# GpSimd subtracts the low half of a gate unit in four operations of two k tiles instead of one over eight

## What is computed

```python
proj = h @ w_in                                   # 1024 x 4772
c_q, c_kv, k_r, fq, fk, fv, f_logit, u, gate_logits = jnp.split(proj, split_points, axis=-1)
o_mla = causal_block_attention(q_mla, k_mla, v_mla)
o_fox = causal_block_attention(q_fox, k_fox, v_fox, cum_log_f)
o_s5 = s5_branch(u, ...)
branches = jnp.stack([o_mla, o_fox, o_s5], axis=2)
gates = jax.nn.sigmoid(gate_logits.reshape(bsz, seq, N_BRANCHES, D_MODEL))
projected = jnp.einsum('bsnw,nwd->bsnd', branches, w_branch)
merged = jnp.einsum('bsnd,bsnd->bsd', gates, projected)
return merged @ w_out
```

## Time and profile before

| | us |
|---|---|
| median of 3 runs (1450.96 to 1451.15) | 1451.15 |
| the profiled execution | 1450.45 |
| its span | 1448.4 |
| TensorE busy | 1429.4 (99%) |
| VectorE busy | 984.3 (68%) |
| ScalarE busy | 664.5 (46%) |
| GpSimd busy | 158.1 (11%), of it line 739: 60.0 |

### The profile page before, as it was taken

The page is one execution under the profiler, slowest core; times in us unless marked ns, Lnnn a source line. Parts: engine busy times, 40 slices in busy tenths (PEclk is TensorE's granted clock), DMA queues, the critical chain, the costliest instruction groups (busy, mean ns, idle before and its releaser), DMA issues.

```text
span 1448.4 us, 19055 instructions
## 1 busy us (share of the span) xinstructions
PE 1429.4 (99%) x7078; PEld 1202.5 (83%) x7078; DVE 984.3 (68%) x1432; ACT 664.5 (46%) x1076; POOL 158.1 (11%) x163
## 2 busy tenths in 40 slices
PE   9999999999999999999999999999999999999998
PEld 7999988888788888888888888888888888888887
DVE  6213556646866557839827688877778886678886
ACT  6231455646445542136512455555555555544332
POOL 1000610112361112103100000000000000000000
PEclk9999999999999999999999999999999999999999
DMA  7102021150121133337561222222222222890222
GB/s 267 64 0 102 19 74 44 52 164 24 46 60 52 37 88 95 82 134 249 185 222 54 88 73 88 87 88 82 71 82 88 88 88 89 318 387 35 95 74 80
DMA packets 130438, 148.94 MB, mean 103 GB/s; under 512 B 11370, under 2 KB 95261, under 8 KB 130077
## 3 DMA queue, kind: packets, MB, share of 16 engines
q1 hardware_dynamic: 130160, 147.68, 30.8%
q10 hardware_dynamic: 189, 0.08, 0.0%
HBM read 110.83 MB, written 36.31 MB: 102 GB/s over the span
## 4 chain that ended last, share of the span: by engine, by line
PE 90%; DVE 5%; ACT 2%; DMA 1%; issue 1%; POOL 1%; SPq 1%; ACTq 0%; DVEq 0%
PE ps L2215 29%; PE ps L693 14%; PE ps L2522 5%; PE ps L2524 5%; PE ps L2523 5%; PE ps L2613 4%; PE ps L374 3%; PE ps L375 3%; PE ps L376 3%; PE ps L882 2%; PE ps L3093 2%; PE ps L3094 2%; PE ps L3095 2%; PE ps L1524 2%; PE ps L861 2%
## 5 line engine op out<-in xcount | busy, mean ns | idle before, releaser
L2215 PE MATMUL ps<-split_arena 128*128 128x512 f32 x1320 | 306.8, 390 | 0.0
L693 PE MATMUL ps<-split_arena 128*128 128x512 f32 x1152 | 290.3, 399 | 2.2 <-ACT plain_arena L728 2.2
L2215 PEld LDWEIGHTS ps<-split_arena 128*128 128x128 f32 x1320 | 247.6, 188 | 51.4 <-issue 0.3
L693 PEld LDWEIGHTS ps<-split_arena 128*128 128x128 f32 x1152 | 208.8, 189 | 42.8 <-issue 3.7
L2398 ACT ACTIVATE down_ops<-down_all 128x1024 fp32r<-128x1024 f32 x77 | 81.5, 1061 | 115.5 <-PE ps L2524 114.9
L2215 PE MATMUL ps<-up_b,split_arena 128*128 128x512 f32 x528 | 126.5, 389 | 0.0
L2417 DVE TENSOR_TENSOR down_ops<-down_all,down_ops 128x1024 fp32r<-128x1024 f32 x77 | 94.1, 1223 | 46.2 <-ACT down_ops L2398 46.0
L2522 PE MATMUL ps<-down_ops 128*128 128x512 f32 x308 | 120.1, 390 | 0.5 <-DVE down_ops L2417 0.5
L2524 PE MATMUL ps<-down_ops 128*128 128x512 f32 x308 | 120.0, 389 | 0.0
L2523 PE MATMUL ps<-down_ops 128*128 128x512 f32 x308 | 120.0, 389 | 0.0
L2215 PEld LDWEIGHTS ps<-up_b,split_arena 128*128 128x128 f32 x528 | 99.2, 188 | 20.5
(11 more groups left out here) (408 smaller groups left out, 2464.1 us busy)
## 6 DMA issues: line engine op xcount, KB each, us to landing
plain_arena<-in_w_in SPq DMA_DIRECT2D x24, 512.0 KB, 4.0
scr_gate<-plain_arena SPq DMA_DIRECT2D x48, 256.0 KB, 2.0
plain_arena<-scr_gate SPq DMA_DIRECT2D x24, 512.0 KB, 4.1
plain_arena<-in_w_up SPq DMA_DIRECT2D x22, 512.0 KB, 5.2
up_raw<-in_w_up SPq DMA_DIRECT2D x22, 512.0 KB, 4.7
scr_act<-plain_arena SPq DMA_DIRECT2D x22, 512.0 KB, 2.6
down_all<-scr_act SPq DMA_DIRECT2D x18, 512.0 KB, 9.1
down_all<-in_w_down SPq DMA_DIRECT2D x18, 512.0 KB, 9.9
```

The costliest lines, as they stand in the source:

```text
L693: mm = nc.tensor.matmul(m.ps[:, self.banks[half], :], w[:, k, :], src[:, k, h * BANK:(h + 1) * BANK], start=(j == 0), stop=(j == self.PER_ ...
L2215: mm = nc.tensor.matmul(o, self.w[j][w][:, k, :], self.h[j][k][h], start=(j in self.OPENS and k == 0 and n == 0), stop=(k == self.HK - 1 a ...
```

## The change

Before, GpSimd subtracted the high half from the weights over all eight k tiles in one operation of 128 x 1024. After it, a loop makes four operations of two k tiles each (128 x 256), in order, and the last of them alone raises the semaphore.

```diff
         for u in range(self.split, min(self.split + n, self.count)):
             pool.wait_ge(self.hi, u + 1)
 
-            self.m.nc.gpsimd.tensor_tensor(self.w_lo[u % 2], self.raw, f32(self.w_hi[u % 2]), ALU.subtract).then_inc(self.lo, 1)
+            for k in range(0, KD, 2):
+                part = slice(k, k + 2)
+                low = self.m.nc.gpsimd.tensor_tensor(self.w_lo[u % 2][:, part], self.raw[:, part], f32(self.w_hi[u % 2][:, part]), ALU.subtract)
+            low.then_inc(self.lo, 1)
         self.split += n
```

## The result

The changed kernel took 1455.72 us (median), the kernel before 1451.15 us: a ratio of 1.0032, 95% interval 1.0022 to 1.0042. The forecast was 1455.5 us. The profiled execution took 1455.55 us around a span of 1453.8 us, so the two traces differ by 5.1 us (5.4 in the span).

The account below looks back on a forecast made before the run. TensorE, 90% of the span, was taken as the bound, so GpSimd counts only where TensorE waits for it. Terms -1.6 - 0.2 + 0.45 + 4.8 + 0.9 = +4.35 us on 1451.15 gave 1455.5 us, range 1450.5 to 1459.5.

Parts of the forecast that it names:

- opening of the FoX attention: Unit 1's low half, with SP's store and ScalarE's copy behind it, all on the path: +0.45 us.
- other normalizations: VectorE normalizations beside line 739, such as 0.95 us at 297.59 against 0.62 at 437.87; booked -0.2 us.
- opening of the MLA attention: VectorE's line 1026 waits for the first part only, ending near 386.4 instead of 388.04: -1.6 us, booked whole.
- s5, units 18 and 19: TensorE waits for two late low halves and the copies behind them: +1.9, +0.3, +2.3, +0.3; sum 4.8 us.
- s5, unit 23: Low half meets VectorE's line 1984 and followers; TensorE waits 0 to 1.2 us for it, taken as +0.9.
- Alternation: Where GpSimd and VectorE shut each other out, they take turns part by part, both directions; forecast's chance 0.65.
- The rival that GpSimd holds on: VectorE gets in only after all four parts; only FoX's opening pays: +0.4, 1451.6 us; chance 0.17.
- The rival on the gain side: s5 operations on two SBUF inputs stay out between parts, normalizations get in: -2.25 us, 1448.9 us; chance 0.11.
- The first wait: s5 stage: TensorE waits for unit 18's low half, 3.65 us late against 1.76 us of slack: +1.9 us.
- The second wait: s5 stage: TensorE, done at 563.3, waits for unit 19's low half, ready at 565.6 at the latest: +2.3 us.
- The ring: s5 loop of low half, SP's load then store, ScalarE's copy and split: 9.2 us, now 12.85 against TensorE's 10.92.
- Units whose cost I called hidden: 18 other units, 0.44 us each, hidden by filler work; in s5, unit 22's lateness of 0.45 to 1.6 us.

## Why the prediction was right, and where it was not

The time came within 0.3 us, by medians (+4.57, forecast +4.35). That it is so near is in part luck. The terms were read in a trace, and by the traces the change costs 5.1 us (5.4 in the span), 0.7 to 1.0 more than the sum. The medians hide about half a microsecond of it: the kernel before loses time to falls of the clock in some four of ten executions, and its profiled execution, which has none, lies 0.70 us under its median, that of the changed kernel only 0.17 under its own. The forecast had no term for the clock in either kernel. Term by term, from TensorE's lateness in the two traces:

| step | forecast | trace |
|---|---|---|
| opening of the FoX attention | +0.45 | +0.56 |
| other normalizations | -0.2 | +0.41 at 257.5, +0.22 at 464 |
| opening of the MLA attention | -1.6 | -1.1 |
| ScalarE's copy behind it | 0 | +0.39 at 411 |
| s5, units 18 and 19 | +4.8 | +4.4 |
| s5, unit 23 | +0.9 | +0.3 |
| sum | +4.35 | +5.3 with 0.1 from the start |

*Alternation, the step on which all rests.* Right: 1.77 us for each of VectorE's operations, three of them between four parts, 7.03 us for the low half. The rival that GpSimd holds on is excluded by these rows; by the Trainium skill (GPSIMD Engine Reference, section 2.1 Instruction dispatch) a core starts the next instruction as soon as it has finished its share of the last, and this trace shows that VectorE got in all the same. The rival on the gain side needed the s5 operations to stay out; they did not.

*The s5 stage.* The first wait was 2.26 us, not 1.9: GpSimd waited 1.03 us for line 1924 at its start (547.14 - 546.11), where line 1921 had cost it 0.58. The second wait was right in kind and size, as the run with parts in the s5 units alone shows (1.98 us), but in the changed kernel's own trace the fall of the clock stands in its place. That the sum was near is no proof of that term; the experiments are. The ring was named with one of its two links: in the changed kernel SP's store and ScalarE's copy do carry the lateness on, as I said, but with the store moved ahead the load carries nearly all of it (a ring of 12.55 us in place of 13.80).

*The opening of the MLA attention.* The normalization and the first wait came out as said (1.6 us). The step that failed is "I book it whole": 0.51 us was given back 4 us later, because the last of the four parts stood in front of another operation of VectorE.

*Other normalizations.* Wrong in sign. At 257.58 the normalization was issued when the fourth part was about to start, and waited for the whole of it (0.98 us, before 0.56, when it met the last third of a microsecond of the single operation). Four parts end 0.44 us later than one, so an operation that used to slip in behind now meets the last part. At 464 the same happened (0.99 against 0.57 us).

*Units whose cost I called hidden.* Nearly right. In the attention only ScalarE's copy at 411 was late: SP had reached a block of small transfers 1.1 us later than before (389.74 against 388.60), so the gain at MLA's opening did not reach the copy. In the second s5 part unit 22 was hidden and unit 23 cost a third of what I had booked.

## What to carry to other kernels

When two engines exclude each other on the same memory and both run chains, the number of pieces decides who loses: cut an operation into n pieces and each boundary lets one whole operation of the other side in, here 1.2 to 1.4 us a boundary. Cut where the other engine is the one waited for (one unit of 24 here), leave whole where the cut operation's own end has little slack, and compare lateness with slack before adding up costs. If the pieces must stay, a wait of the other engine ahead of its chain costs nothing as long as that chain has slack; look where the chain then meets the next pieces (here units 20 and 23). And where a kernel has executions with and without a fall of the clock, compare a trace with executions of its own kind before explaining a median by it.

## What the hardware showed that I had not expected

**The clock.** Behind waits of 1.93 (two traces), 1.94, 2.26 and 2.28 us TensorE's granted clock fell to 1.2 GHz for about 3.5 us; behind waits of 1.78, 1.89, 1.93 (two traces), 1.98 and 2.19 us it did not. Such a fall took 1.6 us in the s5 stage (48 matmuls in 565.73 - 553.20 = 12.53 us instead of 10.92), time that a wait would have taken there anyway; at MLA's opening, where only a short wait stands behind it, it cost 0.7 to 0.9 us. The mean clock shows such a fall in some four of ten executions of the kernel before and in none of the 66 of the six kernels in which that wait is shortened and none over 1.4 us is left.

**Who is shut out.** VectorE's operations that read one of two inputs from TensorE's results (in PSUM) did not wait for the parts. Line 1973 reads them and took 1.22 us at 608.67, with parts running from 607.69 to 610.53, and line 1974, whose inputs both lie in SBUF, took 1.69 us right behind it:

```profile
607.69 2.84 POOL L741 TENSOR_TENSOR split_arena<-plain_arena,split_arena 128x256 fp32r<-128x256 f32 x4 [23.47 <-ACT split_arena L717]
...
608.67 1.22 DVE L1973 TENSOR_TENSOR plain_arena<-ps,plain_arena 128x1024 f32<-128x1024 f32 x1
609.92 1.69 DVE L1974 TENSOR_TENSOR plain_arena<-plain_arena 128x1024 f32<-128x1024 f32 x1
```

The Trainium skill (SBUF — State Buffer, section Who interferes with whom) says that a VectorE instruction with two inputs in SBUF contends with a GpSimd instruction that reads SBUF, and one with at most one such input, outside certain fast modes, does not; both rows agree. One input in SBUF is no safeguard in this kernel: the normalization (TENSOR_SCALAR, one tensor read from SBUF) did wait for a part, 0.98 us at 257.58 against 0.42 alone.
